# Delta rule with three chunks in work, each in two PSUM banks, products of half blocks, and the backward keys and values turned round on TensorE

## Chip, cores and metric

One NeuronCore of a Trainium2 chip runs the whole program. The metric is the device time of one execution in microseconds (us); lower is better. Engines are named PE (TensorE; PEld is its weight load), DVE (VectorE), ACT (ScalarE), POOL (GpSimd) and SP (SyncE, which here only issues DMAs).

## The reference, cut to what matters

The program computes two blocks over 1024 tokens of width 1024: the first has two layers of gated scans and differential attention, the second has neighbourhood attention and a gated delta rule over 256 context and 1024 latent tokens. The change touches the delta rule alone. For each of 8 heads of width 64, in both directions, it takes chunks of 64 tokens:

```python
def _gdn_chunked(q, k, v, g, beta, s0):
    ...
    gc = jnp.cumsum(g, axis=-1)
    ...
    decay = jnp.exp(jnp.where(incl, gc[..., :, None] - gc[..., None, :], -jnp.inf))
    kb = k * beta[..., None]
    lower = jnp.where(strict, jnp.einsum('bnhid,bnhjd->bnhij', kb, k) * decay, 0.0)
    a_mat = lower + jnp.eye(C, dtype=f32)
    rhs = jnp.concatenate([v * beta[..., None], kb * jnp.exp(gc)[..., None]], axis=-1)
    sol = lax.linalg.triangular_solve(a_mat, rhs, left_side=True, lower=True, unit_diagonal=True)
    ...
    def step(S, xs):
        qk_i, qd_i, kd_i, u_i, w_i, gt_i = xs
        v_new = u_i - jnp.einsum('bhck,bhkv->bhcv', w_i, S)
        o_i = jnp.einsum('bhck,bhkv->bhcv', qd_i, S) + jnp.einsum('bhij,bhjv->bhiv', qk_i, v_new)
        S = S * gt_i[..., None, None] + jnp.einsum('bhck,bhcv->bhkv', kd_i, v_new)
        return S, o_i
```

The backward direction runs the same on tokens in reverse order. Context and latents make 20 chunks of 64 tokens in each direction. Only `step` carries state from one chunk to the next; all ahead of it is free of the other chunks.

## The kernel before

The program is a row of stages with a barrier between them; an engine's order is the order in which each stage's generator functions (`sp`, `pe`, `dve`, `act`, `pool`) issue. The stage in question is the class `Delta`, the last but one; `Merge2` follows it. All data are fp32.

**Layout.** A chunk holds the forward direction in partitions 0 to 63 and the backward one in 64 to 127 (`HALVES`), 8 heads beside each other in 512 columns. A product for all heads is 16 matmuls of 64x64 on quarters of the array: `places` yields direction `r`, head parity `par` and head pair `j`, and the tile position says which half of the rows is read and which half of the columns is written. The trace records each such fp32 matmul as two MATMULs and two weight loads, so a product is 32 records. In the backward half the tokens stand in their natural order, and masks for that half are mirrored.

**Steps of a chunk.** SP loads q, k, v into `x` and beta and g into `gb` (line 1893 to 1895). DVE makes `gm` (g under the mask) and `kb` (2059 to 2062). PE sums the gates (1968 to 1971), ACT takes exponentials into `ex`, `gt` and `dec` (2132 to 2135), PE transposes k, kb, q and qg (1977), ACT and DVE copy these to `tk` and `tq` (2138, 2139, 2068). PE scores (1984). DVE multiplies by the decay to `lt`, to its first level `ct[0]` and to `qk` (2073 to 2076). POOL masks `lt` to five further levels `ct[1]` to `ct[5]` (1920). PE turns `ct[0]` in two ways (1991, 1996), and DVE begins the inverse `xm` and its transpose `xt` (2081, 2083).

**Rounds.** Five rounds double the block that is inverted. In round i PE makes y = `ct[i+1]` times `xm` (psum<-delta_xm,delta_ct in the trace; the first name is the moving operand, the second the stationary one), ACT copies it negated to `ym` (2148), PE makes the two corrections (psum<-delta_ym,delta_xt and psum<-delta_xt,delta_ym), and DVE adds them to `xm` (2091) and `xt` (2094). The last round is made by lines 2015 and 2016, and copied by ACT (2152). All of it works on whole 64x64 blocks, of which half is zero.

**Advance.** Then come u and w (psum<-delta_vb,delta_xt and line 1950), and with the state `sm`: `ws`, `qs`, `vn`, `grown`, `inner` (1957, 2108, 1950, 1942), with the state's decay and sum on DVE (2113, 2115) and the output `o` (2165, 2118), stored by ACT.

**Order.** Each chunk of a pair has four PSUM banks, so the two fill all eight. `pairs` weaves the steps of two chunks before it advances both; no step of the next pair stands ahead of that on any engine.

## Time and profile before

| what | value |
|---|---|
| median of 3 runs | 5065.49 us (5064.41 to 5068.58) |
| the profiled execution | 5063.13 us, of which its span 5061.3 us |
| busy in the span | PE 3443.0 us (68%), PEld 2818.5 (56%), DVE 2363.0 (47%), ACT 1236.1 (24%), POOL 962.1 (19%) |
| mean granted clock of TensorE | 0.823 |

The span runs from the first to the last instruction. The stages follow each other with barriers, so a stage's own time adds to the whole. The delta stage stands from 4028 to 4694 us. A row of the timeline gives the start, the time, the engine (a trailing q is the engine's queue, which issues DMAs), the line, the operation with what it writes and reads, and how many like records are merged; in brackets stands the idle time before and what ended it. "issue" is idle time in which the engine waited for nothing that the profile shows.

### The profile page before, as it was taken

The numbers are of one execution on the slowest core, as the hardware profiler recorded it, in microseconds if no ns is written. First come the engines' busy times: TensorE is split into PE (matmuls) and PEld (weight loads), VectorE is DVE, ScalarE is ACT, GpSimd is POOL, SyncE is SP. The second block draws the span as 40 slices with busy tenths as digits, with TensorE's granted clock in tenths as the row PEclk, the third lists the DMA queues.
The fourth block names the chain that finished last, engine by engine and source line by source line (L and its number), as shares of the span: only waits on it lengthen the run. The fifth ranks groups of instructions, "written<-read, shape, count | busy, mean of one in ns | idle before, by whom it ended". The sixth has DMA issues, their size and how long they took to land. (4 is left out here: it accounts for less than half of the span.)

```text
span 5061.3 us, 74737 instructions
## 1 busy us (share of the span) xinstructions
PE 3443.0 (68%) x31808; PEld 2818.5 (56%) x31808; DVE 2363.0 (47%) x3815; ACT 1236.1 (24%) x2052; POOL 962.1 (19%) x761
## 2 busy tenths in 40 slices
PE   5996555665779955457575989951555577777588
PEld 4996443343379944435335989940444466666233
DVE  3114884574621168857553101134767555445333
ACT  2112330242311133214232101111333222222222
POOL 1111441010011133310001112201111033333100
PEclk9997556897889966669887999975767699889789
DMA  3321003422322210031232212224221111111421
GB/s 121 103 93 44 20 20 118 125 70 95 114 95 93 82 33 22 11 111 34 96 121 87 90 68 91 91 89 183 85 77 55 34 37 37 35 34 24 167 81 44
DMA packets 244972, 383.33 MB, mean 76 GB/s; under 512 B 48224, under 2 KB 188440, under 8 KB 243229
## 3 DMA queue, kind: packets, MB, share of 16 engines
q1 hardware_dynamic: 146218, 253.10, 15.6%
q10 hardware_dynamic: 98422, 125.45, 7.2%
q8 instruction: 252, 4.13, 0.4%
q14 instruction: 80, 0.65, 0.0%
HBM read 261.61 MB, written 123.03 MB: 76 GB/s over the span
## 5 line engine op out<-in xcount | busy, mean ns | idle before, releaser
L350 PE MATMUL psum<-proj_w_low,h_high 128*128 128x344 f32 (+1 forms) x2016 | 664.5, 330 | 54.0 <-POOL proj_w_low L334 54.0
L350 PE MATMUL psum<-proj_w_high,h_high 128*128 128x344 f32 (+1 forms) x2016 | 662.9, 329 | 0.0
L350 PE MATMUL psum<-proj_w_high,h_low 128*128 128x344 f32 (+1 forms) x2016 | 662.5, 329 | 0.0
L369 DVE COPY proj_y<-psum 128x344 f32<-128x344 f32 (+1 forms) x126 | 67.8, 538 | 920.9 <-PE psum L350 920.9
L350 PEld LDWEIGHTS psum<-proj_w_low,h_high 128*128 128x128 f32 x2016 | 380.4, 189 | 58.6 <-issue 55.1
L350 PEld LDWEIGHTS psum<-proj_w_high,h_low 128*128 128x128 f32 x2016 | 380.1, 189 | 3.9
L350 PEld LDWEIGHTS psum<-proj_w_high,h_high 128*128 128x128 f32 x2016 | 380.2, 189 | 3.7
L334 POOL TENSOR_TENSOR proj_w_low<-proj_raw,proj_cut 128x2752 fp32r<-128x2752 f32 (+1 forms) x30 | 193.3, 6444 | 974.2 <-DVE proj_cut L363 974.2
L393 ACT ACTIVATE proj_y<-psum 128x344 f32<-128x344 f32 (+1 forms) x126 | 59.3, 471 | 732.0 <-PE psum L350 732.0
L1247 PE MATMUL psum<-merge_wo,merge_yt 128*128 128x512 f32 x512 | 228.3, 605 | 13.5 <-ACT merge_yt L1192 10.0
L1527 PE MATMUL psum<-na_kk,na_q 64*128 64x512 f32 (+2 forms) x320 | 86.9, 693 | 187.0 <-DMA na_v<-proj 99.8
L950 PE MATMUL psum<-diff_kk,diff_q 64*128 64x512 f32 x512 | 136.3, 653 | 104.3 <-ACT diff_w L1033 71.1
L1033 ACT ACTIVATE diff_w<-psum,diff_nm 128x1024 f32<-128x1024 f32 x128 | 142.7, 1114 | 242.5 <-DVE diff_nm L1003 234.2
L350 PE MATMUL psum<-proj_latents_w_low,h_high 128*128 128x448 f32 x512 | 188.2, 368 | 20.1 <-POOL proj_latents_w_low L334 20.1
L525 PE MATMUL psum<-scan_mqs,scan_mks 64*128 64x128 f32 (+1 forms) x2048 | 162.0, 381 | 50.1 <-DVE scan_am L651 45.3
L350 PE MATMUL psum<-roj_latents_w_high,h_high 128*128 128x448 f32 x512 | 188.0, 367 | 0.0
L350 PE MATMUL psum<-roj_latents_w_high,h_low 128*128 128x448 f32 x512 | 187.8, 367 | 0.0
L525 PEld LDWEIGHTS psum<-scan_mqs,scan_mks 64*128 64x128 f32 (+1 forms) x2048 | 144.0, 278 | 69.5 <-issue 60.3
L1247 PEld LDWEIGHTS psum<-merge_wo,merge_yt 128*128 128x128 f32 x512 | 97.8, 194 | 134.8 <-issue 117.7
L651 DVE COPY_PREDICATED scan_am<-scan_lmask,psum 128x512 f32<-128x512 uint32 x224 | 162.5, 726 | 16.4 <-PE psum L525 10.6
L1552 PE MATMUL psum<-ident,na_sc 128*128 128x128 f32 x416 | 78.0, 341 | 134.6 <-ACT na_wt L1637 123.7
L1527 PEld LDWEIGHTS psum<-na_kk,na_q 64*128 64x128 f32 x320 | 43.6, 283 | 221.2 <-DMA na_v<-proj 100.2
(418 smaller groups left out, 7357.3 us busy)
## 6 DMA issues: line engine op xcount, KB each, us to landing
proj_raw<-in_w_in SPq DMA_DIRECT2D x24, 1376.0 KB, 6.8
proj<-proj_y ACTq DMA_DIRECT2D x192, 172.0 KB, 1.9
dn_prep_x<-proj SPq DMA_DIRECT2D x24, 768.0 KB, 11.6
delta_x<-dn_qkv SPq DMA_DIRECT2D x40, 384.0 KB, 4.1
proj_latents_raw<-in_w_in SPq DMA_DIRECT2D x8, 1792.0 KB, 7.3
proj<-proj_latents_y ACTq DMA_DIRECT2D x64, 224.0 KB, 1.9
proj<-proj_y ACTq DMA_DIRECT2D x60, 216.0 KB, 1.9
norm_x<-x_stream SPq DMA_DIRECT2D x24, 512.0 KB, 3.2
```

Of the source, the lines that this page charges most:

```text
L334: G.tensor_tensor(self.wl[:, c % 2], self.raw[:], self.cut[:], ALU.subtract).then_inc(*self.low.inc())
L350: last = PE.matmul(self.ps[:, j % 4, 0:self.width], hp[:, kt, tokens], wp[:, c % 2, kt, :], start=kt == 0 and n == 0, stop=kt == KT - 1 an ...
L369: V.tensor_copy(self.y[:, j % 4, :], self.ps[:, j % 4, 0:self.width]).then_inc(*self.copied[1].inc())
L393: S.activation(self.y[:, j % 4, :], self.ps[:, j % 4, 0:self.width], ACT.Copy).then_inc(*self.copied[0].inc())
L525: last = PE.matmul(out, mk[rows, l, tile, :], mq[rows, l, tile, :], start=True, stop=True, tile_position=(rows.start, 0))
L651: placed = V.copy_predicated(dst, mask.bitcast(U32), sc)
L950: last = PE.matmul(ps[:, 2 * cc + half, :], self.q[rows, s, t * P:(t + 1) * P], self.kk[rows, s, half * 512:(half + 1) * 512], start=True, ...
L1033: S.activation(self.w[:, z, cc], self.both(cc), ACT.Exp, bias=self.nm[:, z, cc:cc + 1], scale=0.125, accum_out=self.sm[:, z, cc:cc + 1]).t ...
L1247: last = PE.matmul(ps[:, 4 * s + 2 + half], self.yt[:, s, j * P:(j + 1) * P], self.wo[:, j, half * 512:(half + 1) * 512], start=j == 0, st ...
L1527: last = PE.matmul(ps[:, 2 * h + b, at:at + width], self.q[rows, g, t * P:(t + 1) * P], self.kk[rows, g, c0:c0 + width], start=True, stop= ...
L1552: last = PE.transpose(ps[:, 4 + j // 4, j % 4 * P:j % 4 * P + P], self.sc[:, n % 2, j * P:(j + 1) * P], self.ident[:])
```

## The change

`Delta` is written anew, with the same mathematics:

- **Three sets** of buffers instead of two, each with two PSUM banks; banks 6 and 7 belong to the step with the state. The programs of all 20 chunks are merged by due time: the steps of a chunk have times 0 to 20.75, and the next chunk's stand 6 later (`PACE`), so some three and a half chunks are under way.
- **Gates** of all chunks are loaded ahead, by 80 DMAs, into one tile `gates`, and their backward half is turned round by one matmul with a reversing matrix (`tri[:, 8]`).
- **Keys and values** of the backward half are turned round by two matmuls per chunk (64x512 each) and copied back into `x` by ACT (`placed`). Both halves are then lower triangular; q stays in natural order, and gets a gate sum of its own (`sums[:, 3]`, `ex[:, 16:24]`).
- **Half blocks.** y, and both corrections, are made only where they are not zero: 32 moving columns instead of 64, read in runs of 2, 4, 8, 16 or 32 (`side`). The stationary operand stays 64x64. The level's mask is applied with the sign when y is copied (`minus`), by DVE instead of ACT; `ym` has a buffer per round. The five masks on POOL go away. Additions to `xm` and `xt` take 256 elements instead of 512.
- **Other moves:** `tq`'s copy of q and `wt` go from DVE to ACT; the state's decay goes from DVE to POOL (`faded`); turning `ct` takes 24 matmuls instead of 32; w is made ahead of u.

```diff
     N = T2 // 64
+    SETS = 3
     HALVES = (slice(0, 64), slice(64, P))
     ROUNDS = 5
+    PACE = 6
 
...
+        self.gates = t("gates", [P, N, 16])
...
+        self.tq, self.tk, self.lt, self.qk, self.ct = sets("tq", 4, 3, P), sets("tk", 4, P), sets("lt", 512), sets("qk", 512), sets("ct", 512)
+        self.xm, self.xt, self.ym = sets("xm", 512), sets("xt", 512), [sets(f"ym{i}_", 512) for i in range(R)]
+        self.um, self.wt, self.vn, self.o = sets("um", 512), sets("wt", 2, 256), sets("vn", 512), sets("o", 512)
+        self.minus = t("minus", [P, R, 256])
...
-    def pairs(self, solve, advance):
-        for c in range(0, self.N, 2):
-            yield from weave(solve(c), solve(c + 1))
-            yield from advance(c)
-            yield from advance(c + 1)
...
+    def side(t, i, s):
+
+        return t.rearrange("p (n s u) -> p n s u", s=2, u=2 << i)[:, :, s]
...
+    def packed(t, i):
+
+        return t.rearrange("p (n u) -> p n u", u=2 << i)
...
+    def sides(t, i, s):
+
+        return t.rearrange("p (b n s u) -> p b n s u", b=2, s=2, u=2 << i)[:, :, :, s]
...
+    def banks(self, c):
+
+        return 2 * (c % self.SETS)
...
+    def chunks(self, program):
+        return by_time(*(paced(program(c), self.PACE * c, 1) for c in range(self.N)))
+
...
-            s = c % 2
-            x, gb, loaded = self.x[s], self.gb[s], self.loaded[s]
-            if c >= 2:
-                SP.wait_ge(*self.scaled_q(c - 2))
-                SP.wait_ge(*self.decayed(c - 2))
-                SP.wait_ge(*self.turned(c - 2))
-            for j, first in enumerate((c * 64, CTX + 64 * (N - 1 - c))):
-                rows, tokens = self.HALVES[j], slice(first, first + 64)
-                SP.dma_start(x[rows], self.dn[tokens, :]).then_inc(*loaded.inc())
-                SP.dma_start(gb[rows, 0:8], self.dg[tokens, 8 * j:8 * j + 8]).then_inc(*loaded.inc())
-                SP.dma_start(gb[rows, 8:16], self.dg[tokens, 16 + 8 * j:24 + 8 * j]).then_inc(*loaded.inc())
-            yield
+            at, back = self.dg[c * 64:c * 64 + 64], self.dg[self.back(c):self.back(c) + 64]
+            for rows, t, first in ((self.HALVES[0], at, 0), (self.HALVES[1], back, 8)):
+                SP.dma_start(self.gates[rows, c, 0:8], t[:, first:first + 8]).then_inc(*self.gated_in.inc())
+                SP.dma_start(self.gates[rows, c, 8:16], t[:, 16 + first:24 + first]).then_inc(*self.gated_in.inc())
+        yield from self.chunks(self.sp_chunk)
+
+    def back(self, c):
+
+        return CTX + 64 * (self.N - 1 - c)
...
+    def sp_chunk(self, c):
+        SP, Z, s = self.nc.sync, self.SETS, c % self.SETS
+        yield -8
+        if c >= Z:
+            SP.wait_ge(*self.scaled_q(c - Z))
+            SP.wait_ge(*self.decayed(c - Z))
+            SP.wait_ge(*self.turned_q(c - Z))
+        for first, rows in zip((c * 64, self.back(c)), self.HALVES):
+            SP.dma_start(self.x[s][rows], self.dn[first:first + 64]).then_inc(*self.loaded[s].inc())
...
+    def mm(self, out, i, o, left, right, start=True, stop=True):
+
+        return self.nc.tensor.matmul(out, left, right, start=start, stop=stop, tile_position=(64 * i, 64 * o))
...
+        yield 0
+        PE.wait_ge(*self.loaded[s](2 * (c // Z) + 1))
+        if c >= Z:
+            PE.wait_ge(*self.u_copied(c - Z))
+        if c == 0:
+            PE.wait_ge(*self.gates_placed(0))
+        self.mm(ps[H[1], B, :], 1, 1, self.tri[H[1], 8], x[H[1], 512:1024])
+        self.mm(ps[H[1], B + 1, :], 1, 1, self.tri[H[1], 8], x[H[1], 1024:1536]).then_inc(*self.mirrored.inc())
...
-        near, far = B + 2, B
         for i in range(R):
-            near, far = far, near
-            PE.wait_ge(*self.xm_ready(self.turn(c, i, R)))
-            PE.wait_ge(*self.levels(R * c + i))
-            self.product(near, ct[:, i + 1], xm, dst=1).then_inc(*self.y_made.inc())
-            yield
-            PE.wait_ge(*self.y_copied(self.turn(c, i, R)))
-            PE.wait_ge(*self.xt_ready(self.turn(c, i, R)))
+            yield 6 + 2 * i
+            if i == 0:
+                PE.wait_ge(*self.begun(c))
+            else:
+                PE.wait_ge(*self.updated[i - 1](c))
+            for r, par, j in self.places():
+                rows, o = H[r], r ^ par
+                last = self.mm(packed(at(o, col(B + par, 0, j, 32)), i), r, o, grp(self.lt[s])(rows, par, j), side(grp(xm)(rows, par, j), i, 0))
+            last.then_inc(*self.y_made[i].inc())
+            yield 7 + 2 * i
+            PE.wait_ge(*self.y_copied[i](c))
             if i < R - 1:
-                self.product(far, xt, ym, src=1).then_inc(*self.x_fix.inc())
-                self.product(near, ym, xt, src=1, dst=1).then_inc(*self.xt_fix.inc())
-                yield
-        for r, par, j, cols in self.places():
-            swapped, rows = self.HALVES[r ^ par], self.HALVES[r]
-            out, at = ps[rows, near + par, 64 * j:64 * j + 64], (64 * (r ^ par), 64 * r)
-            PE.matmul(out, eye[swapped], xt[swapped, cols], start=True, stop=False, tile_position=at)
-            last = PE.matmul(out, ym[swapped, cols], xt[swapped, cols], start=False, stop=True, tile_position=at)
-        last.then_inc(*self.xt_fix.inc())
-        yield
+                for r, par, j in self.places():
+                    h, rows = r ^ par, H[r ^ par]
+                    self.mm(packed(at(r, col(B + par, 128, j, 32)), i), h, r, grp(xt)(rows, par, j), side(grp(ym[i])(rows, par, j), i, 0))
+                for r, par, j in self.places():
+                    h, rows = r ^ par, H[r ^ par]
+                    last = self.mm(packed(at(h, col(B, 256 + 128 * par, j, 32)), i), h, h, grp(ym[i])(rows, par, j), side(grp(xt)(rows, par, j), i, 1))
+            else:
+                for r, par, j in self.places():
+                    h, rows = r ^ par, H[r ^ par]
+                    out = at(r, col(B + par, 0, j, 64))
+                    self.mm(out, h, r, eye[rows], grp(xt)(rows, par, j), stop=False)
+                    last = self.mm(side(out, i, 1), h, r, grp(ym[i])(rows, par, j), side(grp(xt)(rows, par, j), i, 1), start=False)
+            last.then_inc(*self.fixed[i].inc())
...
+        A, sm, wt = 2 * Z, self.sm, self.wt[s]
+        yield 18
         if c:
             PE.wait_ge(*self.state(c - 1))
-        self.with_state(B, lambda hr, r, dr, j: wt[hr, r, 64 * j:64 * j + 64]).then_inc(*self.ws.inc())
-        self.with_state(B + 2, lambda hr, r, dr, j: tq[hr, j, 2, dr]).then_inc(*self.qs.inc())
+            PE.wait_ge(*self.o_added(c - 1))
+        for r, par, j in self.places():
+            self.mm(at(r, col(A + par, 256, j, 64)), par, r, tq[H[par], j, 2, H[r]], sm[H[par], r, 64 * j:64 * j + 64])
+        for r, par, j in self.places():
+            last = self.mm(at(r, col(A + par, 0, j, 64)), par, r, wt[H[par], r, 64 * j:64 * j + 64], sm[H[par], r, 64 * j:64 * j + 64])
+        last.then_inc(*self.ws.inc())
...
+        for i in range(self.ROUNDS):
+            last = V.tensor_copy(self.minus[:, i].rearrange("p (h d) -> p h d", h=4), bc(self.tri[:, i + 2].unsqueeze(1), [P, 4, 64]))
+        self.k.vo.chain(last)
+        yield from self.chunks(self.dve_chunk)
...
+        V.tensor_tensor(h3(xm[:]), self.mask(7), h3(ps[:, B, :]), ALU.subtract)
+        V.tensor_tensor(h3(xt[:])[:, 0:4], four, h3(ct[:])[:, 0:4], ALU.subtract)
+        V.tensor_tensor(h3(xt[:])[:, 4:8], four, ps[:, B + 1, 0:256].rearrange("p (h d) -> p h d", h=4), ALU.subtract).then_inc(*self.begun.inc())
+        V.wait_ge(*self.begun(c))
+        for i in range(R):
+            small = lambda t: t.rearrange("p b (n u) -> p b n u", u=2 << i)
+            yield 6.5 + 2 * i
+            V.wait_ge(*self.y_made[i](c))
+            minus = bc(self.side(self.minus[:, i], i, 0).unsqueeze(1), [P, 2, 64 >> i, 2 << i])
+            V.tensor_tensor(sides(self.ym[i][s][:], i, 0), small(ps[:, B:B + 2, 0:128]), minus, ALU.mult).then_inc(*self.y_copied[i].inc())
+            yield 7.5 + 2 * i
+            if i == R - 1:
+                break
+            V.wait_ge(*self.fixed[i](c))
+            left, right = sides(xm[:], i, 0), sides(xt[:], i, 1)
+            V.tensor_tensor(left, left, small(ps[:, B:B + 2, 128:256]), ALU.add)
+            V.tensor_tensor(right, right, ps[:, B, 256:512].rearrange("p (b n u) -> p b n u", b=2, u=2 << i), ALU.add).then_inc(*self.updated[i].inc())
+            V.wait_ge(*self.updated[i](c))
...
+        S.activation(self.gates[back].rearrange("p c g -> p (c g)"), self.ps[back, 0, 0:16 * self.N], ACT.Copy).then_inc(*self.gates_placed.inc())
...
+        yield 0.25
+        S.wait_ge(*self.mirrored(c))
+        S.activation(self.x[s][H[1], 512:1536], ps[H[1], B:B + 2, :].rearrange("p b d -> p (b d)"), ACT.Copy).then_inc(*self.placed.inc())
...
+        S.activation(tq[:, :, 1:3].rearrange("p j b t -> p b j t"), ps[:, B:B + 2, :].rearrange("p b (j t) -> p b j t", j=4), ACT.Copy).then_inc(*self.copied_q.inc())
```

How PE's order changes in the rounds. In the kernel before, the rows of a round of two chunks (names end in buffer numbers):

```order
L1942 MATMUL psum<-delta_xm_281_27477,delta_ct_279_27475 64x64 x16
L1942 MATMUL psum<-delta_xm_282_27478,delta_ct_280_27476 64x64 x16
L1942 MATMUL psum<-delta_ym_285_27481,delta_xt_283_27479 64x64 x16
L1942 MATMUL psum<-delta_xt_283_27479,delta_ym_285_27481 64x64 x16
L1942 MATMUL psum<-delta_ym_286_27482,delta_xt_284_27480 64x64 x16
L1942 MATMUL psum<-delta_xt_284_27480,delta_ym_286_27482 64x64 x16
```

No step of another stage of work stands between them. After the change, PE from the state's products of a chunk to the sums of the chunk that enters, in the middle of the stage:

```order
L1988 MATMUL psum<-delta_sm_27442,delta_tq_282_27478 64x64 x16
L1988 MATMUL psum<-delta_sm_27442,delta_wt_321_27517 64x64 x16
L1988 MATMUL psum<-delta_xm_298_27494,delta_lt_289_27485 64x32 x16
L1988 MATMUL psum<-delta_xm_299_27495,delta_lt_290_27486 64x32 x16
L1988 MATMUL psum<-delta_x_248_27444,delta_tri_27441 64x512 x2
L1988 MATMUL psum<-delta_vn_324_27520,delta_kd_279_27475 64x64 x16
L1988 MATMUL psum<-delta_ym_1_313_27509,delta_xt_301_27497 64x32 x16
L1988 MATMUL psum<-delta_xt_301_27497,delta_ym_1_313_27509 64x32 x16
L1988 MATMUL psum<-delta_ym_2_305_27501,delta_xt_302_27498 64x32 x16
L1988 MATMUL psum<-delta_xt_302_27498,delta_ym_2_305_27501 64x32 x16
L2007 MATMUL psum<-delta_gm_251_27447,delta_sums_27440 128x512
```

The rounds of one chunk (xm 299, xt 302), those of an older one (xm 298, xt 301) and the state's products (sm, vn) now alternate with the first steps of a new chunk (x 248, gm 251); the products of the rounds read 64x32.

On DVE in the kernel before, the updates of the rounds of two chunks:

```order
L2091 TENSOR_TENSOR delta_xm_281_27477<-delta_xm_281_27477,psum 128x2x4x64
L2094 TENSOR_TENSOR delta_xt_283_27479<-delta_xt_283_27479,psum 128x2x4x64
L2091 TENSOR_TENSOR delta_xm_282_27478<-delta_xm_282_27478,psum 128x2x4x64
L2094 TENSOR_TENSOR delta_xt_284_27480<-delta_xt_284_27480,psum 128x2x4x64
L2091 TENSOR_TENSOR delta_xm_281_27477<-delta_xm_281_27477,psum 128x2x4x64
```

They stand alone. After the change, DVE from a chunk's `vn` to the next updates:

```order
L2165 TENSOR_TENSOR delta_vn_325_27521<-delta_um_319_27515,psum 128x512
L2153 TENSOR_TENSOR delta_ym_2_314_27510<-psum,delta_minus_27526 128x16x16
L2153 TENSOR_TENSOR delta_ym_0_303_27499<-psum,delta_minus_27526 128x128x2
L2121 COPY delta_gd_255_27451<-delta_gates_27462 64x8
L2122 COPY delta_gd_255_27451<-delta_gates_27462 64x8
L2123 TENSOR_TENSOR delta_gm_252_27448<-delta_tri_27441,delta_gates_27462 128x512
L2124 TENSOR_TENSOR delta_kb_268_27464<-delta_x_249_27445,delta_gates_27462 128x512
L2169 TENSOR_TENSOR delta_sm_27442<-delta_faded_27443,psum 128x512
L2159 TENSOR_TENSOR delta_xm_299_27495<-delta_xm_299_27495,psum 128x16x16
L2160 TENSOR_TENSOR delta_xt_302_27498<-delta_xt_302_27498,psum 128x16x16
L2159 TENSOR_TENSOR delta_xm_297_27493<-delta_xm_297_27493,psum 128x128x2
L2160 TENSOR_TENSOR delta_xt_300_27496<-delta_xt_300_27496,psum 128x128x2
```

The gate steps of the entering chunk (gd, gm, kb) now stand between the copy of y of one chunk and the sum of the state of another.

On SP at the start of the stage in the kernel before:

```order
L1882 DMA delta_sums_27440<-in_c_sums 128x384
L1883 DMA delta_tri_27441<-in_c_tri 128x512
L1893 DMA delta_x_247_27443<-dn_qkv 64x1536
L1894 DMA delta_gb_249_27445<-dn_gates 64x8
L1895 DMA delta_gb_249_27445<-dn_gates 64x8
L1893 DMA delta_x_247_27443<-dn_qkv 64x1536
```

The first load of `x` is the third DMA. On SP at the same place after the change:

```order
L1926 DMA delta_sums_27440<-in_c_sums 128x512
L1927 DMA delta_tri_27441<-in_c_tri 128x576
L1931 DMA delta_gates_27462<-dn_gates 64x8
L1932 DMA delta_gates_27462<-dn_gates 64x8
L1931 DMA delta_gates_27462<-dn_gates 64x8
L1932 DMA delta_gates_27462<-dn_gates 64x8
```

The four rows of gates shown are the first of 80; all stand ahead of the first load of `x`.

## Rows read from the trace of the kernel before

**Rows 1.** Timeline at both ends of the delta stage: start us, us, engine, line, operation.

```profile
4028.30 0.33 SPq L1882 DMA_DIRECT2D delta_sums<-in_c_sums  x1
...
4029.67 0.60 SPq L1894 DMA_DIRECT2D delta_gb<-dn_gates  x1
4030.31 0.60 SPq L1895 DMA_DIRECT2D delta_gb<-dn_gates  x1
...
4039.30 2.05 PE L1968 MATMUL psum<-delta_gm,delta_sums 128*128 128x512 f32 x2 [14.90 <-DVE delta_kb L2062]
...
4694.10 0.34 SPq L2198 DMA_DIRECT2D merge_nw<-in_dn_norm_w  x1
```

**Rows 2.** Windows: stretch, its length, busy us of PE, PEld, DVE, ACT, POOL (records), clock, DMA.

```profile
4104.50:4169.50 65.00, 45.58 (x1584) 40.90 (x1584) 33.96 (x50) 13.53 (x28) 22.82 (x18) 0.92 0.16 38
...
4258.00:4297.00 39.00, 27.37 (x1271) 25.50 (x1263) 17.11 (x26) 8.66 (x15) 5.02 (x5) 1.00 0.05 11
...
4018.50:4024.50 6.00, 5.91 (x29) 5.72 (x27) 0.84 (x4) 0.60 (x1) 0.00 (x0) 0.50 0.01 3
...
4045.00:4050.00 5.00, 5.00 (x25) 5.00 (x25) 1.91 (x2) 1.79 (x6) 5.00 (x5) 0.50 0.00 0
```

**Rows 3.** Waits from 4040 to 4690 us: us in all, times, longest.

```profile
POOL delta_vb L1909 <- DVE delta_o L2118: 317.0, 18, 32.2
ACT delta_ym L2148 <- PE psum L1942: 270.4, 79, 6.6
...
PEld psum L1942 <- issue: 86.6, 67, 2.9
```

**Rows 4.** Timeline of PE in the rounds of one pair.

```profile
4265.09 0.63 PE L1942 MATMUL psum<-delta_ym,delta_xt 64*64 64x64 f32 x30
4265.56 1.04 PE L1942 MATMUL psum<-delta_xt,delta_ym 64*64 64x64 f32 x30
...
4266.49 0.86 PE L1942 MATMUL psum<-delta_xm,delta_ct 64*64 64x64 f32 x40
```

**Rows 5.** Timeline of PE, records that resume after an idle time called issue.

```profile
4264.46 0.74 PE L1942 MATMUL psum<-delta_xt,delta_ym 64*64 64x64 f32 x19 [0.59 <-issue]
...
4268.20 0.51 PE L1942 MATMUL psum<-delta_xm,delta_ct 64*64 64x64 f32 x19 [0.84 <-issue]
...
4272.26 0.85 PE L1942 MATMUL psum<-delta_xt,delta_ym 64*64 64x64 f32 x22 [1.41 <-issue]
```

**Rows 6.** DMA queue 8 from 4258 to 4297 us: packets, MB, share.

```profile
q8 instruction: 11, 0.18, 2.0%
```

**Rows 7.** The same queue from 4040 to 4690 us.

```profile
q8 instruction: 125, 2.05, 1.4%
```

**Rows 8.** Timeline: weights of 128 columns under 64 and under 128 moving columns, half clock.

```profile
4019.18 5.22 PE L1540 MATMUL psum<-na_v,na_wt 128*128 128x64 f32 x24
...
4047.27 1.06 PE L1977 MATMUL psum<-ident,delta_x 128*128 128x128 f32 x4
...
4048.12 1.06 PE L1977 MATMUL psum<-ident,delta_qg 128*128 128x128 f32 x4
```

**Rows 9.** Groups by line from 4040 to 4690 us: records, busy us, mean ns, idle.

```profile
L1920 POOL TENSOR_TENSOR delta_ct<-delta_lt,delta_tri 128x512 f32<-128x512 f32 x100 | 133.1, 1370 | 18.9 <-DVE delta_lt L2073 18.9
...
L2091 DVE TENSOR_TENSOR delta_xm<-delta_xm,psum 128x512 f32<-128x512 f32 x80 | 54.8, 685 | 77.1 <-PE psum L1942 77.1
...
L2075 DVE TENSOR_TENSOR delta_ct<-delta_lt,delta_tri 128x512 f32<-128x512 f32 x20 | 23.7, 1184 | 0.7
...
L2138 ACT ACTIVATE delta_tk<-psum 128x512 f32<-128x512 f32 x20 | 12.0, 598 | 34.2 <-PE psum L1977 34.2
```

**Rows 10.** Timeline: a DVE copy of 256 columns from PSUM.

```profile
4016.16 0.42 DVE L1600 COPY na_wt<-psum 128x256 f32<-128x256 f32 x1
```

**Rows 11.** The page's costliest groups: a matmul of 512 moving columns.

```profile
L1247 PE MATMUL psum<-merge_wo,merge_yt 128*128 128x512 f32 x512 | 228.3, 605 | 13.5 <-ACT merge_yt L1192 10.0
```

**Rows 12.** DMA issues: each KB, us from issue to landing.

```profile
delta_x<-dn_qkv SPq DMA_DIRECT2D x36, 384.0 KB, 4.1
```

397 lines of the change are left out of this document (188 added, 209 removed).

## The prediction

> **What bounds the kernel now.** Only the delta stage changes, so I read first how long it stands: from SP's first DMA at 4028.3 us to the next stage's first at 4694.1, 665.8 us; PE starts at 4039.3 [rows 1]. Then the windows: a pair of chunks takes 65 us, one after the other, which is 32.5 us a chunk, and in a pair PE is busy for 46 us, DVE for 34, POOL for 23, ACT for 14 [rows 2]. No engine is full. The waits say why: POOL stands until the pair before is done (317 us in all), ACT waits for each y (270 us), PE itself for a reason called issue (86.6 us) [rows 3]. So the stage is a chain of steps with handovers, in which two chunks cover each other badly.
>
> The wait called issue is to be understood, since it stays. In the rounds PE resumes from such a wait at 4264.46, 4268.20 and 4272.26 us [rows 5], every 3.7 to 4.1 us. In that stretch the instruction queue moves 11 packets of 16 KB in 39 us [rows 6], one per 3.5 us. Over the stage it is 125 packets [rows 7] for 20 chunks of 1584 PE instructions (792 matmul records, as many weight loads), 253 instructions each. I read this as a floor: PE gets no more than some 253 instructions in 3.65 us, however short they are.
>
> **What PE does per chunk after the change, at full clock.** In the rounds the clock was at 1.00 [rows 2]. Two rates are seen there. A product whose 16 matmuls use all four quarters of the array runs 30 records in 0.47 us, and y 40 in 0.64 (0.86 less the last one's own 0.22): 15 to 16 ns a record, 0.47 us a product. The product xt,ym uses only the two diagonal quarters: 30 records in 0.83 us or more, 0.9 us a product with its start [rows 4].
> - Thirteen products on four quarters (5 y, 4 corrections of xm, w, two with the state, grown): 13 x 0.47 = 6.1 us; the last round's double one 0.95.
> - Six on the diagonal (4 corrections of xt, u, inner) 5.4; turning ct, now 48 records instead of 64, 1.0.
> - Scoring, 128 columns wide, 0.86 by twice the rate of a product of 64; 16 transposes and the gate sums: transposes took 0.85 us per four at half clock [rows 8], so 0.107 each at full clock, 1.75; sums 0.9 + 4 x 0.21 = 1.7.
> - New: keys and values turned round, two matmuls of 512 columns, four records of 228.3 / 512 = 0.446 us [rows 11], 1.8 us on one quarter.
>
> Sum 19.6 us. It counts the half products at their old price. What speaks for that: with 128 stationary columns, 24 records of 64 moving columns took 5.22 us, 0.21 each, and those of 128 moving columns 0.85 / 4 = 0.21 [rows 8], both at a clock of 0.50 [rows 2]. The weight load sets the pitch there, and the change leaves the stationary side 64x64. The price lies between half (3.5 us less per chunk: 9 x 0.23 + 4 x 0.45, less the last round) and the old one; I take the old one, the row's. The number of PE instructions hardly falls: 399 program matmuls a chunk against 404.
>
> **Waits of PE that stay.** With three and a half chunks merged, I lay PE's order against the handovers, each 0.25 us after PE and 0.2 before it (my reading of the gaps), with DVE at 0.68 for 512 elements and 0.42 for 256 [rows 9, 10], 1.18 for the ct mask, ACT at 0.60 for 512 [rows 9]. PE waits where a chunk's chain is longer than what the other chunks put between:
> - turned keys, then ACT's copy (1.1), DVE's gd, gm, kb (2.1 with handovers), then the sums: 0.5 us;
> - the last round of the older chunk, whose copy of y stands in DVE's queue behind qg and o: 1.1;
> - ACT's copy of q (1.1) ahead of scoring: 0.7;
> - scoring, then lt, ct and qk in two halves on DVE (3.2 us) ahead of turning ct: 1.2;
> - beginning the inverse, 1.5 us on DVE, ahead of the first y: 0.6.
>
> That is 4.1 us, so 23.7 us a chunk. The new chain (turn, copy, gd to kb) is queued on DVE ahead of the state's sum and of two chunks' updates; for those PE has 3.3 us of other work at that place, so it costs only the 0.5.
>
> **Instructions.** 1564 PE instructions are 6.2 packets, 22.6 us at 3.65: less than 23.7, but they are not evenly spread. From grown through both corrections 256 instructions need 2.6 us and must take 3.65, which moves the sums by 0.55 after the wait there is used up; from turning ct to the first y another 1.15 us is lost. With that a chunk takes 25.4; I say **25.5 us** against 32.5.
>
> In a sentence of its own: the Trainium skill, "Runtime: NRT & Kernel Launch", section "Instruction fetch mechanics", has it that crossing a 16 KiB block of instructions is mostly hidden. By that the term would be nil and a chunk 23.7 us, the whole 36 us shorter; rows 5 and 6 speak against it in this stage.
>
> DVE: 15.2 us of operations a chunk (five copies of y and eight updates at 0.42, twelve of about 0.7 to 1.2). ACT and POOL have less. None is the bound. POOL's five masks (5 x 1.37 us [rows 9]) go, hidden now behind PE's rounds but for a few waits, and ACT's y goes; both are inside the 32.5 and not counted again.
>
> **The start and the end.** SP issues a DMA every 0.64 us [rows 1]. 80 loads of gates take 51.2 us, PE's first matmul waits for all of them, and the first x is issued behind them, and lands 4.1 us later [rows 12]. So PE starts at about 57 us into the stage instead of 11: **46 us of loss**, covered by nothing. The pipeline is filled at about the same rate, since a lone chunk's first six steps take 22 us or more by their chain. It must be drained: after the last chunk's first 25.5 us come its rounds beside two older ones (5.2 packets of instructions, 19 us), the rest beside one (12), and the state alone (9): 40 us, where the kernel before has none beyond its last pair.
>
> Sum: 57 + 20 x 25.5 + 40 + 3 for the last store and barrier = 610 us, against 665.8: 55.8 less. From the profiled 5063.1 that is 5007; the median of before lies 2.4 us higher, so **5009 us**.
>
> **Rivals.**
> 1. *Half width is half price.* If moving columns set the pitch of small matmuls, PE's work is 16 us, and the packets bound the chunk: 22.6 to 23.3. Stage 562, time about 4962. For it: 15 ns a record on four quarters is 60 ns on each, which may be the time of the moving columns as well as of the weights [rows 4]. Against it: 64 and 128 moving columns cost the same under equal weights [rows 8].
> 2. *Handovers cost more.* DVE's queue is strict, and operations that read SBUF stretch beside POOL's (gm and ct are above 0.68 now, ct 1184 ns [rows 9]). With 2 us more a chunk, 27.5: stage 650, time 5049.
> 3. *Fine runs are dear, and the kernel is slower.* In rounds 0 and 1 PE reads moving columns, and DVE writes, in runs of 2 and 4 elements. No row shows that. If it doubles y and both corrections of these two rounds, that is 2 x 1.85 = 3.7 us, a chunk takes 29.2, and the stage 684: time 5084. It decides from 28.3 us a chunk on (565.8 / 20), where start and end have eaten the gain.
> 4. *Chunks don't overlap.* The order shows that they do on every engine, so this needs a wait on a buffer: PE may turn keys of chunk c only after u of c - 3 is copied, which stands one slot ahead. Part of rival 2.
>
> On rival 3 the Trainium skill, "SBUF — State Buffer", section "Door 1: The DMA port swizzle", says that two hits per 16-byte line give full bandwidth; runs of two fp32 elements have just that, so by it the rival costs nothing. No row here shows it.
>
> **How the numbers follow.** Forecast (24.3 to 26.7 us a chunk, 4985 to 5033) 0.45; rival 1 (below 4985) 0.2; rivals 2 and 4 (5033 to 5060) 0.2; rival 3 and anything like it above that 0.15. What can be told from no change is 0.2%, 10 us. Below 5055 lies 0.83, within 10 us of 5065 0.05, above 0.12. The range leaves out a tenth at either side: 4960 to 5068. Unknown prices move it by 20 us per us in a chunk.
>
> **What the new profile would show.** SP issues gates until about 4080 us, and PE's first record is at about 4085. From then a turn of keys every 25.5 us. Products x30 still start 0.47 and 0.85 us apart, though 32 wide: if 0.24, rival 1 is right. The instruction queue still moves about 124 packets in the stage, with PE waits called issue. DVE's updates take 0.42 us for runs of 2 as of 32: if rounds 0 and 1 stand out, rival 3. The forecast is wrong if the first PE record comes early, if a chunk takes over 27 us, or if PE's clock does not stay near 1.0 once its prep runs beside rounds (0.92 over a pair now [rows 2]).

## The result: slower by 1.6%, and where the time went

The changed kernel takes 5144.8 us in the median of 4 runs (5133.7 to 5161.9), the kernel before 5065.0 (5056.2 to 5068.6). The ratio is 1.0163, with a 95% interval of 1.0127 to 1.0199: slower by 1.6%, where 5009 us was predicted, in a range up to 5068. The profiled run took 5153.9 us with a span of 5152.1; the span of before was 5061.3.

First the two ends of the stage in the timeline of the changed kernel (start us, us, engine, line, operation), to be held against [rows 1]:

```profile
4039.20 0.33 SPq L1926 DMA_DIRECT2D delta_sums<-in_c_sums  x1
...
4090.43 0.60 SPq L1932 DMA_DIRECT2D delta_gates<-dn_gates  x1
...
4092.48 1.30 PE L1988 MATMUL psum<-delta_gates,delta_tri 64*64 64x320 f32 x2 [57.18 <-DMA delta_gates<-dn_gates]
...
4097.24 1.11 PE L1988 MATMUL psum<-delta_x,delta_tri 64*64 64x512 f32 x1 [3.46 <-DMA delta_x<-dn_qkv]
...
4715.77 1.91 PE L1988 MATMUL psum<-delta_x,delta_tri 64*64 64x512 f32 x4
...
4783.77 0.34 SPq L2257 DMA_DIRECT2D merge_nw<-in_dn_norm_w  x1
```

The stage stands for 744.6 us instead of 665.8. It has three parts. From SP's first DMA to the first turning of keys 58.0 us go (57 predicted). From the first turning to that of the 20th chunk it is 618.5 us, which is 32.55 us for each of 19 chunks (25.5 predicted). From there to the next stage it is 68.0 us (25.5 + 40 + 3 = 68.5 predicted). So the whole miss of 134 us lies in the period: 19 x 7.05. The span grew by 90.8 us, 12.0 more than the stage. Of these, 10.9 lie ahead of the stage, which begins at 4039.2 instead of 4028.3 us. That start moved between 4029.8 and 4048.6 us among the kernels below, which are all alike up to there, and the medians differ by 79.8 us where the two stages differ by 78.8. So it is scatter.

Then the windows of the changed kernel, as in [rows 2]: stretch, length, busy us of PE, PEld, DVE, ACT, POOL (records), granted clock, share of DMA. The first goes from the first product y to the last; the other two are neighbours inside one chunk.

```profile
4124.00:4765.00 641.00, 553.70 (x15267) 479.44 (x15269) 288.19 (x544) 123.36 (x247) 110.62 (x96) 0.74 0.13 30
4268.00:4285.00 17.00, 14.24 (x522) 11.93 (x516) 9.01 (x20) 5.41 (x8) 3.31 (x4) 0.99 0.28 66
4285.00:4298.00 13.00, 12.96 (x264) 11.86 (x266) 5.82 (x10) 1.07 (x5) 2.42 (x3) 0.50 0.01 3
```

TensorE is busy for 86% of the rounds and its clock is 0.74. Before it was busy for 70% of a pair and the clock was 0.92 [rows 2]. In the second window it does 522 records in 17 us, in the third 264 in 13 us without a pause: it has become the bound, and for about half the time it runs at the lower of its two levels, 1.2 GHz. The Trainium skill, "TensorE: Matmul & The Clock Gate", section "HAM oscillation — how this bites in real kernels", lays such a swinging clock to TensorE standing idle between groups of matmuls. This trace does not agree with that as the whole cause: here TensorE idles less than before, and the clock is lower, and in the third window it stays at 0.50 while TensorE is busy for 12.96 of 13.00 us.

Where does it fall? PE's timeline around the change from 0.99 to 0.50:

```profile
4280.35 1.12 PE L1988 MATMUL psum<-delta_xm,delta_lt 64*64 64x32 f32 x64
4281.31 1.91 PE L1988 MATMUL psum<-delta_x,delta_tri 64*64 64x512 f32 x4
4285.04 1.13 PE L1988 MATMUL psum<-delta_vn,delta_kd 64*64 64x64 f32 x32 [1.82 <-ACT delta_o L2224]
```

There the new turning stands: four records of 512 moving columns on one quarter of the array. Right behind it PE waits 1.82 us for ACT's copy of o, ahead of the product that makes the state grow. That wait comes in nearly every chunk (PE's waits, 4124 to 4765 us: us in all, times, longest):

```profile
PE psum L1988 <- issue: 41.2, 35, 3.4
PE psum L1988 <- ACT delta_o L2224: 32.8, 19, 1.8
PE psum L1988 <- DVE delta_qk L2138: 6.8, 12, 0.6
```

The kernel before had that wait too, a little shorter (its PE's waits, 4040 to 4690 us):

```profile
PE psum L1950 <- ACT delta_o L2165: 21.7, 20, 1.9
```

Three suspects for the clock are in this picture: narrow moving operands, the turning on one quarter, and the wait. The experiments below take them one at a time.

### The profile page after: what moved, and what is told of

Its sections match the earlier page's. It is cut to its first block and busy times, and to the rows that moved or that the text cites. A ratio compares the mean times of both kernels' runs of the same rounds, so it can differ in the third digit from the quotient of the medians.

```text
span 5152.1 us, 74060 instructions
## 1 busy us (share of the span) xinstructions
PE 3580.4 (69%) x31610; PEld 2911.1 (57%) x31610; DVE 2338.1 (45%) x3916; ACT 1231.5 (24%) x2033; POOL 848.6 (16%) x681
```

## Two prices first: half width and fine runs

The same products, in the full-clock and in the half-clock part of that chunk (PE's timeline):

```profile
4270.02 0.65 PE L1988 MATMUL psum<-delta_ym,delta_xt 64*64 64x32 f32 x30
...
4270.49 1.09 PE L1988 MATMUL psum<-delta_xt,delta_ym 64*64 64x32 f32 x31
...
4288.42 1.12 PE L1988 MATMUL psum<-delta_ym,delta_xt 64*64 64x32 f32 x30
...
4289.30 1.94 PE L1988 MATMUL psum<-delta_xt,delta_ym 64*64 64x32 f32 x32
```

At full clock a product of 32 moving columns starts 0.47 us ahead of the next, exactly as 64 columns did [rows 4]; at half clock it is 0.88 us. So half width is not half price, and rival 1 is wrong. Rival 3 (fine runs are dear) is wrong on PE: the 64 records of y at 4280.35, shown above, are those of rounds 0 and 3 of two chunks, with runs of 2 and 16 elements, and the turning starts 0.96 us behind them, 15 ns a record. It is wrong on DVE too. DVE's groups, all rounds together (min/median/max ns, first and last start):

```profile
L2153 DVE TENSOR_TENSOR delta_ym<-psum,delta_minus x100: 406/417/426, 4125.3 to 4765.6; 128x256 f32<-128x256 f32 x100
...
L2159 DVE TENSOR_TENSOR delta_xm<-delta_xm,psum x80: 412/421/422, 4132.0 to 4763.0; 128x256 f32<-128x256 f32 x80
...
L2160 DVE TENSOR_TENSOR delta_xt<-delta_xt,psum x80: 411/414/417, 4132.3 to 4763.3; 128x256 f32<-128x256 f32 x80
```

No operation takes over 426 ns, with runs of 2 elements as with runs of 16 or 32.

## Experiment 1: wide products, few loads, and narrow products in the kernel before

`wide` takes 64 moving columns in y and in the correction of xm; DVE then reads every other run of the result. The correction of xt moves to columns 0 to 255 and stays at 32.

```
- last = self.mm(packed(at(o, col(B + par, 0, j, 32)), i), r, o, grp(self.lt[s])(rows, par, j), side(grp(xm)(rows, par, j), i, 0))
+ last = self.mm(at(o, col(B + par, 0, j, 64)), r, o, grp(self.lt[s])(rows, par, j), grp(xm)(rows, par, j))
...
- self.mm(packed(at(r, col(B + par, 128, j, 32)), i), h, r, grp(xt)(rows, par, j), side(grp(ym[i])(rows, par, j), i, 0))
+ self.mm(at(r, col(B + par, 256, j, 64)), h, r, grp(xt)(rows, par, j), grp(ym[i])(rows, par, j))
```

> The changed kernel, but y and the correction of xm take all 64 moving columns again (the unwanted half of each result is not read); the correction of xt stays at 32. Instructions, their order, the waits and what the other engines do are the same. Theory A (the narrow moving operands cost TensorE its full clock: in the changed kernel 351.6 of 619 us between the first and the last turning of keys passed at 0.5, with 59 ns a matmul record, and 267.4 us at 1.0, with 34 ns): the granted clock in the rounds goes back to 0.85 or more, a chunk takes 25 to 28 us instead of 32.6, and the kernel is 90 to 140 us faster than the changed one, about 5010 to 5050 us. Theory B (the clock fell for another reason, such as the order of the work or the 57 us of idle time at the start): clock 0.70 to 0.78 as now and 5130 to 5160 us. Theory C (the clock is not what costs; handovers and DVE's queue are): clock may rise, but the time stays within 20 us of 5145.

`gates4` loads the gates of all chunks with 4 DMAs:

```
+ at, back = (self.dg[a:a + 64 * N].rearrange("(c p) g -> p c g", p=64) for a in (0, CTX))
+ for rows, t, first in ((self.HALVES[0], at, 0), (self.HALVES[1], back[:, ::-1], 8)):
+     SP.dma_start(self.gates[rows, :, 0:8], t[:, :, first:first + 8]).then_inc(*self.gated_in.inc())
+     SP.dma_start(self.gates[rows, :, 8:16], t[:, :, 16 + first:24 + first]).then_inc(*self.gated_in.inc())
```

> The changed kernel with the 80 loads of gates made into 4 (all chunks of one half and one kind in one DMA; the same bytes to the same places). The prediction's term for the start says that 76 issues of 0.64 us, 48 us, lie bare ahead of PE's first matmul: PE starts at about 10 to 15 us into the stage, and the kernel takes 5095 to 5105 us. If the start were hidden by something else (x landing late), it gains less than 15 us. Theory B (the long idle start is why the clock is low in the rounds after it): the clock of the rounds rises from 0.75 to over 0.85 and the gain is 90 us or more; theory A: it stays near 0.75.

> Both edits: 64 moving columns in y and the correction of xm, and 4 loads of gates. Theory A: the two gains add up, 90 to 140 us and 45 us: 4960 to 5010 us, faster than the kernel before. Theory B or C: 5090 to 5105 us, or what the 4 loads alone give.

`before_half` is the kernel before with `right[rows, cols.start:cols.start + width]`, width 32, as the moving operand of y and both corrections. It leaves out the other 32 columns of each result, so it shows only times.

> The kernel before (two chunks, its old order), in which y and both corrections take only the first 32 of 64 moving columns; so the inverse is not computed rightly and the output differs from the reference. Nothing else is changed. Theory A (narrow operands cost the clock): the granted clock of the rounds falls from 1.0 to between 0.5 and 0.8, and since TensorE has more waits here, a pair takes 75 to 90 us instead of 65: slower than before by 50 to 200 us. Theory B: clock and time stay as before, 5055 to 5070 us. If half width is half price, the time falls below 5050 us.

Measured: wide 5115.1 us (ratio to before 1.0084, interval 1.0058 to 1.0111); gates4 5089.7 (1.0041, 1.0024 to 1.0058); both 5067.3 (0.9994, 0.998 to 1.0008); before_half 5098.3 (1.0059, 1.0038 to 1.0081). The windows from the first to the last y, of wide, gates4, both, before_half, and last the kernel before:

```profile
4124.00:4735.00 611.00, 511.82 (x15276) 442.42 (x15269) 289.03 (x545) 123.30 (x247) 110.67 (x96) 0.82 0.13 32
```

```profile
4069.00:4704.00 635.00, 549.11 (x15274) 476.30 (x15274) 289.03 (x546) 123.19 (x247) 110.61 (x96) 0.75 0.13 30
```

```profile
4075.00:4686.00 611.00, 513.31 (x15274) 443.64 (x15274) 288.85 (x546) 123.58 (x247) 110.70 (x96) 0.82 0.14 32
```

```profile
4064.00:4706.00 642.00, 532.74 (x15073) 500.41 (x15068) 313.00 (x451) 128.75 (x261) 213.52 (x169) 0.72 0.13 30
```

```profile
4059.00:4674.00 615.00, 437.89 (x15090) 394.38 (x15084) 310.17 (x451) 126.81 (x261) 213.56 (x169) 0.91 0.13 32
```

The 76 loads that go bring 55 us in the median and 53.9 in the length of the stage (48 expected). The first turning comes 46.2 us sooner (11.8 us into the stage instead of 58.0), the rest is a difference in the rounds and the end. The clock stays at 0.75. So the start costs what was predicted, and is no reason for the clock (theory B falls). Wide products raise the clock to 0.82 and take 42 us off PE's busy time with more columns in the same number of records. In the kernel before, where nothing but the width is changed and no turning of keys stands, the clock falls from 0.91 to 0.72. PE's busy time grows from 438 to 533 us and its idle time falls from 177 to 109, so the rounds take 642 us instead of 615. The kernel is 0.6% slower, some 30 us, less than the 50 to 200 of theory A. So narrow operands do cost clock. But wide gains 30 us where theory A gave 90 to 140, and both edits together end at 5067.3 us, where it gave 4960 to 5010. The clock of 0.82 is not 1.0, and something else holds it down.

## Experiment 2: the turning on the whole array

In the trace of `wide_gates4` the clock still fell once a chunk, at the turning. `turn128` turns keys and values with a 128x128 matrix, the unit matrix in the forward half. It has the same moving columns and as many records.

```
- self.mm(ps[H[1], B, :], 1, 1, self.tri[H[1], 8], x[H[1], 512:1024])
+ PE.matmul(ps[:, B, :], self.sums[:, 4], x[:, 512:1024], start=True, stop=True)
```

> The changed kernel, but keys and values are turned round with a 128x128 matrix (the unit matrix for the forward half, the reversing one for the backward half) instead of 64x64 on one quarter of the array: the same 512 moving columns and the same number of records, so the same time at equal clock, and the same numbers come out where they are read. Seen in the traces so far: the granted clock falls from 1.0 to 0.5 once in every chunk, where the turning of keys and values stands in PE's queue, and comes back some 14 to 17 us later. Theory D (it is the work on one quarter alone, some 2 us of it at a stretch, that costs the clock, and the narrow products keep it down): the clock in the rounds rises from 0.75 to 0.9 or more, and the kernel takes 5020 to 5080 us. Theory A alone (narrow products, not the turning): 0.75 and 5130 to 5150 us. Theory F (it is the sparse stretch of long matmuls, not how much of the array they use): as A.

> The same with the gates in 4 loads. Theory D: 45 to 55 us less than with the turning edit alone, 4970 to 5030 us. Theory A or F: as the 4 loads alone, 5080 to 5100 us.

> Full array for the turning, 64 moving columns in y and the correction of xm, gates in 4 loads. If both the narrow products and the turning on one quarter cost clock, this has the clock at 0.9 to 1.0 from the third chunk on: 20 chunks of 25.6 to 27 us, the prediction's rate, and 4950 to 4990 us. If the turning has nothing to do with it: 5067 us, as without it.

In the last kernel the correction of xt takes its 32 columns twice, so that 64 move, and the next head overwrites the second copy:

```
- last = self.mm(packed(at(h, col(B, 256 + 128 * par, j, 32)), i), h, h, grp(ym[i])(rows, par, j), side(grp(xt)(rows, par, j), i, 1))
+ twice = 1 if n > 13 else 2
+ moving = bc(side(grp(xt)(rows, par, j), i, 1).unsqueeze(1), [64, twice, 16 >> i, 2 << i])
+ out = ps[rows, B, at0:at0 + 32 * twice].rearrange("p (t n u) -> p t n u", t=twice, u=2 << i)
+ last = self.mm(out, h, h, grp(ym[i])(rows, par, j), moving)
```

For the overwriting the 16 matmuls also stand in another order (n, where it was `places`), so this edit changes two things at once.

> As the one before, and the correction of xt takes its 32 columns twice, as 64 moving columns (the second copy is overwritten by the next head). If narrow operands still cost clock there, the clock rises and it is 5 to 40 us faster than the one before; if the clock is already full, the pitch of those products stays at 25 to 29 ns a record (the weight load sets it) and the time is the same within 10 us.

Measured: 5106.5 us (1.0092, 1.0068 to 1.0117); 5065.2 (1.0003, 0.999 to 1.0017); 5031.5 (0.9945, 0.9928 to 0.9962); 5028.4 (0.9929, 0.9912 to 0.9947). The windows of the four, first to last y:

```profile
4118.00:4739.00 621.00, 516.82 (x15272) 450.79 (x15274) 287.75 (x545) 123.30 (x247) 110.72 (x96) 0.82 0.13 31
```

```profile
4087.00:4695.00 608.00, 503.57 (x15262) 439.81 (x15259) 287.52 (x544) 123.24 (x247) 110.70 (x96) 0.84 0.13 32
```

```profile
4071.00:4648.00 577.00, 465.84 (x15260) 406.13 (x15264) 287.41 (x545) 123.38 (x247) 110.69 (x96) 0.92 0.14 34
```

```profile
4080.00:4642.00 562.00, 440.65 (x15262) 383.31 (x15264) 286.65 (x544) 123.70 (x247) 110.74 (x96) 0.97 0.15 34
```

The turning on one quarter costs as much clock as the narrow products: each edit alone gives 0.82, both give 0.92, and with the correction of xt wide too it is 0.97. PE's busy time for the same number of records goes from 554 to 441 us. These 113 us of PE's work are what the changed kernel pays for its clock. Neither theory D (5020 to 5080 us for turn128) nor theory A (5130 to 5150) met the 5106.5 measured, and turn128_wide_gates4 was expected at 4950 to 4990: a chunk still takes 28.3 us in the last kernel, not 25.5 to 27. What the clock gave back came out in part as waits: PE is idle for 121 us of 562 now, and for 87 of 641 in the changed kernel. PE's waits of the last kernel, 4080 to 4642 us:

```profile
PE psum L1987 <- issue: 55.5, 47, 3.1
PE psum L1987 <- ACT delta_o L2226: 32.7, 19, 1.8
PE psum L1987 <- DVE delta_ym L2155: 19.2, 20, 1.1
PE psum L1987 <- DVE delta_qk L2140: 6.9, 10, 1.6
```

The wait for ACT's copy of o is as long as in the changed kernel. In the code v_new is made by DVE, o is copied by ACT only after that (both read the same two PSUM banks), and PE's next product waits for both, with only a few steps of other chunks ahead of it.

## Experiment 3: the growth of the state half a slot later, other pace, more instructions

`late_grown` starts from the fastest kernel so far:

```
- yield 19
+ yield 19.5
  PE.wait_ge(*self.v_new(c))
...
- yield 20
+ yield 20.5
  PE.wait_ge(*self.state(c))
...
- yield 19.5
+ yield 19.75
  V.wait_ge(*self.grown(c))
...
- yield 20.5
+ yield 20.75
  V.wait_ge(*self.inner(c))
```

(and ACT's store of o at 20.9.) `pace7` has PACE = 7. `pad252` asks for 12 waits on a semaphore long reached ahead of each of a chunk's 21 steps on PE.

> From the fastest kernel so far (full-array turning, wide products, 4 loads of gates; 5028 us, clock 1.00 over most of the rounds, and yet 28.3 us a chunk). What is moved: the growth of the state on PE, and the sums behind it on DVE and ACT, stand half a slot later in the queues, behind the other chunks' steps of that slot. In the trace of that kernel PE waits 11.6 us in 200 for ACT's copy of o ahead of this product, 1.7 us a chunk, and 7.1 us for DVE's copy of y in the last round. Theory H (handovers with too little queued between them are part of what was under-sized at full clock): 1.0 to 2.5 us a chunk less, 20 to 50 us, 4980 to 5010 us. Theory P (instruction packets alone set the pace at full clock): the same time within 10 us, since the waits called issue grow by what this one loses.

> The fastest kernel so far with a new chunk every 7 slots instead of 6, so exactly three in work instead of three and a half, and fewer steps of others between a chunk's own. Theory H: the waits for DVE and ACT grow by more than 1 us a chunk, and the kernel is 20 to 80 us slower (5050 to 5110 us). Theory P: 5020 to 5040 us.

> The fastest kernel so far with 252 more instructions a chunk on PE, 12 ahead of each of its 21 steps: waits on a semaphore that has long been reached, so they hold nothing up but must be fetched, one packet of 16 KB more a chunk, 7.1 instead of 6.1. By the prediction's floor (3.65 us for 253 instructions) 7.1 packets need 26 us and fit in the 28.3: the waits cost only their own execution, under 10 us in all. Theory P (each packet stalls PE by the 1.1 us that the waits called issue last now): 22 us or more, 5050 us or above.

Measured: late_grown 4967.1 us (0.9811, 0.9791 to 0.9832); pace7 5050.5 (0.9978, 0.9966 to 0.999); pad252 5099.6 (1.0076, 1.0052 to 1.0101). Window and PE's waits of late_grown:

```profile
4077.00:4587.00 510.00, 438.64 (x15242) 381.10 (x15242) 286.26 (x544) 123.33 (x247) 109.58 (x95) 0.96 0.16 38
```

```profile
PE psum L1987 <- issue: 42.8, 40, 3.3
PE psum L2006 <- DVE delta_kb L2126: 13.5, 19, 1.8
PE psum L1987 <- DVE delta_qk L2140: 7.4, 11, 1.6
PE psum L1987 <- DVE delta_xt L2148: 2.9, 4, 1.5
PE psum L1987 <- DVE delta_ym L2155: 2.4, 4, 1.1
```

PE's busy time is the same (439 us), and its idle time falls from 121 to 71 us. The waits for o are gone, those for y shrink from 19.2 to 2.4. A chunk takes 25.75 us (first turning at 4050.84, that of the 20th chunk at 4540.02). The median is 61 us below that of turn128_allwide_gates4, and 1.9% below the kernel before. That was theory H, with more than it had promised.

pace7 is 22 us slower than turn128_allwide_gates4, the low end of theory H, but not by its mechanism. Window, first to last y, and PE's waits between 4200 and 4600 us, which are now for DVE's preparation:

```profile
4071.00:4656.00 585.00, 476.94 (x15274) 415.61 (x15274) 275.51 (x545) 124.37 (x247) 111.67 (x96) 0.90 0.14 33
```

```profile
PE psum L2006 <- DVE delta_kb L2126: 27.6, 13, 2.1
PE psum L1987 <- issue: 18.6, 19, 3.6
PE psum L1987 <- DVE delta_qk L2140: 17.1, 9, 2.1
```

PE is idle for 108 us instead of 121, and busy for 477 instead of 441, with the clock at 0.90 instead of 0.97. So the whole loss is clock, with wide products and the turning on the whole array: another order of work costs clock too, and which part of it does is not shown.

pad252 doesn't tell what it was made for. The page of its kernel and that of the kernel it starts from:

```profile
span 5090.5 us, 76504 instructions
```

```profile
span 5028.3 us, 73984 instructions
```

Only 126 instructions a chunk came on top, not 252. The instruction queue over the stage (packets, MB, share) of pad252 and of its base:

```profile
q8 instruction: 132, 2.16, 1.4%
```

```profile
q8 instruction: 122, 2.00, 1.4%
```

The stage grew by 67.6 us. At 1.1 us a packet, the length of a wait called issue, 10 packets would be 11 us; the rest would be the waits' own time, some 22 ns each (an estimate: 56.6 us over 2520 waits). Nothing here separates the two, so the price of a packet stays open.

## Experiment 4: is the clock a cause by itself?

late_grown was built on three earlier edits: wide products, the turning on the whole array, and 4 loads of gates. `late_only` is the changed kernel with the shift of late_grown alone; `late_narrow` and `late_quarter` put one suspect back into late_grown.

> The changed kernel with one edit: the growth of the state and the sums behind it half a slot later. Narrow products, turning on one quarter and 80 loads of gates stay. If the clock is a cause by itself (theory A with D): the granted clock in the rounds stays at 0.7 to 0.8, a chunk at 30 to 32 us, and the kernel at 5080 to 5140 us. If the wait for ACT's copy of o was the root (TensorE idle there, and the clock fell for that): the clock rises to 0.9 or more, a chunk takes 26 us, and the kernel 5010 to 5030 us.

> The fastest kernel so far (4967 us) with the narrow products of the changed kernel back, 32 moving columns in y and both corrections. If narrow operands cost the clock even where PE waits little: clock 0.75 to 0.9 and 5010 to 5050 us, at least 40 us slower. If they cost only beside the waits: within 15 us of 4967.

> The fastest kernel so far with the turning on one quarter of the array back. If that costs the clock by itself: a fall of the clock in most chunks at the turning, 0.8 to 0.9 in the rounds, and 5000 to 5040 us. If it costs only beside the waits: within 15 us of 4967.

Measured: late_only 5059.5 us (0.9991, 0.998 to 1.0001); late_narrow 4978.9 (0.983, 0.9815 to 0.9845); late_quarter 4971.5 (0.9814, 0.9796 to 0.9833). Their windows, first to last y:

```profile
4115.00:4665.00 550.00, 483.07 (x15225) 424.94 (x15222) 282.30 (x543) 123.30 (x247) 109.63 (x95) 0.86 0.15 35
```

```profile
4082.00:4605.00 523.00, 452.19 (x15215) 392.42 (x15218) 285.36 (x544) 123.09 (x247) 109.59 (x95) 0.93 0.16 37
```

```profile
4071.00:4579.00 508.00, 434.17 (x15242) 381.64 (x15242) 285.74 (x544) 123.22 (x247) 109.59 (x95) 0.96 0.16 38
```

late_only lies between its two theories (5080 to 5140, and 5010 to 5030 us); late_narrow and late_quarter came out as "only beside the waits", within 15 us of late_grown. With the wait gone and all else as in the changed kernel the clock goes from 0.74 to 0.86 and the kernel is 85 us faster. Only 33 us of that were waits for o: in the rounds the idle time falls by 20 us and the busy time by 71, which is clock. Once the wait is gone, narrow products alone cost 12 us, and the turning on one quarter nothing that can be told (4 us, the intervals overlap). Both together, with the wait gone, still hold the clock at 0.86. So in the new order each of the three costs clock beside the others, and less or nothing alone. In the changed kernel and in wide_gates4 the fall stands where they meet, at the turning ahead of the wait. It needs neither the turning (before_half, 0.72) nor narrow products (pace7, 0.90), so these three are not all that can bring it about.

All in one table, each clock and length from one profiled run (us per chunk is the mean distance of the turnings of chunks 0 and 19; clock, busy and idle time of PE from the first to the last y):

| kernel | clock | PE busy | PE idle | us a chunk | stage | median |
|---|---|---|---|---|---|---|
| kernel before | 0.91 | 438 | 177 | 32.5 | 665.8 | 5065.0 |
| before_half | 0.72 | 533 | 109 | – | 692.0 | 5098.3 |
| changed kernel | 0.74 | 554 | 87 | 32.6 | 744.6 | 5144.8 |
| wide | 0.82 | 512 | 99 | 30.9 | 710.1 | 5115.1 |
| gates4 | 0.75 | 549 | 86 | 31.8 | 690.7 | 5089.7 |
| wide_gates4 | 0.82 | 513 | 98 | 30.8 | 662.8 | 5067.3 |
| turn128 | 0.82 | 517 | 104 | 31.1 | 724.4 | 5106.5 |
| turn128_gates4 | 0.84 | 504 | 104 | 30.9 | 661.0 | 5065.2 |
| turn128_wide_gates4 | 0.92 | 466 | 111 | 29.3 | 629.4 | 5031.5 |
| turn128_allwide_gates4 | 0.97 | 441 | 121 | 28.3 | 618.5 | 5028.4 |
| pace7 | 0.90 | 477 | 108 | 29.8 | 637.3 | 5050.5 |
| pad252 | 0.95 | 495 | 136 | 31.6 | 686.2 | 5099.6 |
| late_grown | 0.96 | 439 | 71 | 25.8 | 566.5 | 4967.1 |
| late_only | 0.86 | 483 | 67 | 27.9 | 653.9 | 5059.5 |
| late_narrow | 0.93 | 452 | 71 | 26.5 | 578.0 | 4978.9 |
| late_quarter | 0.96 | 434 | 74 | 25.7 | 564.8 | 4971.5 |

## Why the prediction was wrong, point by point

- **The start (57 us) and the end (40 + 3 us behind the last chunk's first period)** were right: 58.0 and 68.0 us against 57 and 68.5, and in gates4 the first turning comes 46.2 us sooner, against the 46 us that were laid to the loads of gates.
- **The price of half width** was right: 0.47 us a product at full clock, as with 64 columns.
- **The period, 25.5 us a chunk, is the step that failed**, by 7.05 us, 134 us in all. The step is "What PE does per chunk after the change, at full clock": it took PE's work at a clock of 1.00, and the rounds ran at 0.74. Per chunk (the stretch of rounds holds 15267 of some 782 records a chunk, so 19.5 chunks) PE is busy for 28.4 us and idle for 4.5 (together 32.9, as the stretch leaves out the quicker ends). Predicted were 19.6 and 5.9. The window of rows 2 with a clock of 1.00 was taken from an old order of work, which had wide operands and no turning, and was carried over to a new one. That the forecast falls "if PE's clock does not stay near 1.0" stood in the last lines, but no case had it as its mechanism and no chance was given to it. It is 5.9 us of the period: 28.4 less the 22.5 that late_grown's PE takes at 0.96. (That kernel also has wide products and the turning on the whole array, which at equal clock take no longer, as the last section shows.)
- **PE's work itself** was short too. Two and three quarter chunks of late_grown ran at full clock throughout:

```profile
4232.00:4303.00 71.00, 61.05 (x2163) 53.51 (x2152) 41.74 (x78) 19.11 (x39) 17.30 (x15) 1.00 0.20 48
```

That is 28.2 ns a record, 22.1 us for the 782 of a chunk, where the sum has 19.6. That the sum took each product at its pitch, without its own last 0.2 us where a wait follows, is a likely reason, but no run tests it. (In the last step of the sum 5007.3 and 2.4 make 5010, not 5009, which changes nothing.)
- **The five dependency waits (4.1 us)** lacked the largest: the growth of the state waiting for v_new and then for ACT's copy of o, 1.7 us in nearly every chunk. It stood in the trace of before, 21.7 us in 20 waits, and that row was not drawn on. Those that were listed are small in the changed kernel: qk ahead of turning ct takes 6.8 us in 641, and DVE's copy of y 2.5. All waits of PE that are not called issue come to 46 us in 641, 2.4 us a chunk, so the 4.1 was too much. Rival 2 said that handovers cost 2 us a chunk more; directly they cost less than was counted, and what the wait for o cost through the clock was larger (late_only: 71 us of busy time).
- **The instruction term (1.7 us)** is about right in size: waits called issue are 41.2 us in 641 in the changed kernel, 2.1 us a chunk, and the queue moved 122 packets in the stage as against 125 before [rows 7], 6.1 a chunk. Whether it is a floor or a stall of its own at each packet was not settled.
- **The sum at full clock was nearly right by errors that offset one another, which is luck.** With the clock at 0.96 and the wait for o gone a chunk takes 25.75 us: PE is busy for 2.9 us more than was predicted and idle for 3.7 instead of 5.9. By the prediction's own sum, with 4 loads of gates in place of 80, the stage would be 610 less 48, 562 us; late_grown has 566.5.
- **The overlap of three and a half chunks does pay**, as predicted, where the clock holds: late_grown has the same chunks in work and is 1.9% faster than the kernel before. No run takes the overlap apart from the other moves of the change.

## To carry to other kernels

An estimate from full-clock durations holds only if the new order keeps the clock, so look not just at whether TensorE is busy but at what it is busy with: here narrow moving operands, and long matmuls on one quarter of the array ahead of a short wait, went with a clock that fell to half, and it stayed there for 13 us in which TensorE never paused. A cut of moving columns that doesn't lower the pitch brought nothing here and cost clock. Where several such places meet a handover wait, try the wait first: moving one step half a slot gave 85 us here, more than wide (30) or turn128 (38). And of a pipelined order list every product's waits, also the short chain that carries the state from chunk to chunk.
